# Sums of query and key squares of the first attention from a high and a low part, with later sums and products

## The reference, cut to what matters

```
proj = h @ w_in
qkv = silu(causal_depthwise_conv(proj[..., :3 * A_INNER], conv_w))
q = l2_norm(q) * (A_HEAD_DIM ** -0.5)      # 16 heads of 128 channels
k = l2_norm(k)                             # x * rsqrt(sum(x * x) + eps)
...                                        # beta and decay by token and head
lower = where(tri_strict, einsum(k * beta, k) * decay, 0)     # key-key
qk = einsum(q, k) * decay                                      # query-key
sol = triangular_solve(eye + lower, ...)
```

## Time and profile before

| What | Value |
|---|---|
| Time of the profiled execution | 1381.22 us |
| Its span | 1379.4 us |
| TensorE (PE) busy | 1361.8 us, 99% |
| VectorE (DVE) busy | 973.0 us, 71% |
| ScalarE (ACT) busy | 792.3 us, 57% |
| GpSimd (POOL) busy | 47.2 us, 3% |
| TensorE's share of the chain that ended last | 87% |
| Granted clock of TensorE, mean | 1.00 |
| Bytes moved | 305.80 MB, mean 222 GB/s |

### The profile page before, as it was taken

How to read it: one execution, slowest core, us unless ns; L and a number is a source line. 1 busy time by engine, 2 the same in 40 slices (tenths; PEclk the granted TensorE clock), 3 DMA queues, 4 the chain that set the end, 5 groups by cost and what they waited for, 6 DMA issues and landing times.

```text
span 1379.4 us, 20382 instructions
## 1 busy us (share of the span) xinstructions
PE 1361.8 (99%) x7803; PEld 1158.8 (84%) x7803; DVE 973.0 (71%) x1259; ACT 792.3 (57%) x1021; POOL 47.2 (3%) x93
## 2 busy tenths in 40 slices
PE   6999999999999999999999999999999999999999
PEld 2446999888888888888999988888888888888887
DVE  3568989977787888799765558765666655656552
ACT  2215435465787787745888775467556566466431
POOL 0000022000000000000000000000000000000000
PEclk9999999999999999999999999999999999999999
DMA  9999899856476656474644656645555556555562
GB/s 383 409 417 372 343 379 409 302 188 208 140 264 209 191 182 221 163 237 153 193 149 133 215 175 218 206 163 187 181 183 180 170 171 207 166 175 175 176 191 84
DMA packets 79109, 305.80 MB, mean 222 GB/s; under 512 B 8928, under 2 KB 9328, under 8 KB 74544
## 3 DMA queue, kind: packets, MB, share of 16 engines
q1 hardware_dynamic: 67824, 261.30, 55.1%
q0 software_dynamic: 11200, 43.31, 9.0%
HBM read 294.07 MB, written 12.60 MB: 222 GB/s over the span
## 4 chain that ended last, share of the span: by engine, by line
PE 87%; DMA 6%; DVE 4%; ACT 2%; issue 1%; SPq 0%; POOL 0%; DVEq 0%; ACTq 0%; POOLq 0%
PE acc L713 42%; PE acc L715 21%; DMA raw<-weights 3%; PE acc L738 3%; PE misc L738 3%; PE misc L966 3%; PE acc L657 2%; PE acc L656 2%; PE acc L658 2%; DMA mod_ring<-mod_w 1%; DMA gate_ring<-weights 1%; PE misc L873 1%; DVE w_lo L1604 1%; PE misc L864 1%; DVE gate_ring L1574 1%
## 5 line engine op out<-in xcount | busy, mean ns | idle before, releaser
L713 PE MATMUL acc<-b_op,w_hi 128*128 128x512 f32 x1792 | 635.0, 398 | 0.0
L1604 DVE TENSOR_TENSOR w_lo<-raw,w_hi 128x1024 fp32r<-128x1024 f32 x392 | 470.8, 1221 | 211.6 <-ACT w_hi L1134 206.9
L1134 ACT ACTIVATE w_hi<-raw 128x1024 fp32r<-128x1024 f32 x392 | 404.1, 1053 | 229.7 <-PE acc L715 116.4
L715 PE MATMUL acc<-b_op,w_lo 128*128 128x256 f32 x1792 | 499.6, 279 | 0.0
L713 PEld LDWEIGHTS acc<-b_op,w_hi 128*128 128x128 f32 x1792 | 336.3, 188 | 77.1 <-DVE vo L1648 0.2
L715 PEld LDWEIGHTS acc<-b_op,w_lo 128*128 128x128 f32 x1792 | 337.6, 188 | 0.5
L713 PE MATMUL acc<-a_op,w_hi 128*128 128x512 f32 x760 | 265.0, 395 | 0.3 <-DVEq L1784 0.3
L715 PE MATMUL acc<-a_op,w_lo 128*128 128x256 f32 x760 | 210.8, 277 | 0.0
L713 PEld LDWEIGHTS acc<-a_op,w_hi 128*128 128x128 f32 x760 | 142.5, 188 | 33.8 <-DVEq L1784 0.6
L715 PEld LDWEIGHTS acc<-a_op,w_lo 128*128 128x128 f32 x760 | 142.8, 188 | 0.1
L1574 DVE CUSTOM_DVE_ANT_0 mod_ring<-mod_ring,silu_b,vecs 128x2048 f32<-128x2048 f32 x26 | 61.1, 2350 | 47.6 <-DMA mod_ring<-mod_w 47.4
(11 more groups left out here) (258 smaller groups left out, 1750.1 us busy)
## 6 DMA issues: line engine op xcount, KB each, us to landing
raw<-weights SPq DMA_DIRECT2D x392, 512.0 KB, 4.4
mod_ring<-mod_w SPq DMA_DIRECT2D x26, 1024.0 KB, 13.5
u_ring<-weights SPq DMA_DIRECT2D x32, 512.0 KB, 13.6
gate_ring<-weights POOLq DMA_DIRECT2D x30, 512.0 KB, 8.5
mod_late<-mod_w SPq DMA_DIRECT2D x6, 1024.0 KB, 7.5
xres<-x_t SPq DMA_DIRECT2D x4, 512.0 KB, 15.9
xres<-x_t POOLq DMA_DIRECT2D x4, 512.0 KB, 9.1
sums_b<-sums_d POOLq DMA_DIRECT2D x8, 256.0 KB, 4.6
```

The source lines that it names most:

```text
L713: nc.tensor.matmul(to, w_hi[:, slot, ch], op[:, kt], start=kt == 0, stop=False, skip_group_check=True)
L715: last = nc.tensor.matmul(to[:, 0:T], w_lo[:, slot, ch], op[:, kt, 0:T], start=False, stop=kt == KT - 1, skip_group_check=True)
L1134: nc.scalar.activation(w_hi[:, m.c % HL_SLOTS], raw[:, q.c % RAW_SLOTS], ACT.Copy).then_inc(own.up(s_hi), 1)
L1604: nc.vector.tensor_tensor(w_lo[:, slot], raw[:, q.c % RAW_SLOTS], w_hi[:, slot].bitcast(F32), ALU.subtract).then_inc(own.up(s_lo), 1)
```

## The change

The sums of squares of the queries (c = 0, 2, 4, 6) and of the keys in passes 0 to 2 (c = 1, 3, 5) are made from two fp32r parts. ScalarE copies the squares `t2` to `qk_hi` right behind the Square; VectorE subtracts (heads_low) and writes the rest over `t2` as `t2_lo`; TensorE multiplies both with `ones_r` (sums_of_parts, 4 times hi and lo). The last key sums (c = 7) stay as they were. `ones_r` is made ahead of the passes and no longer ahead of the second attention.

TensorE does the query sums after slab 6 (before: 5) and key_query after slab 3 (2). In passes 0 to 2 it does the key sums after slab 4 (3) and key_key after slab 7 (6); in pass 3 these two stay at 3 and 6. VectorE does the l_t products of passes 0 to 2 in the next pass, behind its first low part; those of pass 3 stay where they were. Its first low part of the second group goes ahead of the product for `q_n`. heads_low stands behind the eviction of the keys' first half (queries), and behind the second low part of the second group (keys).

```diff
+        t2_lo = at("t2_lo", [P, 4 * T], F32R, t2_at)
+        qk_hi = at("qk_hi", [P, 4 * T], F32R, vo_at + 32 * T)
...
-            def split_sums(n):
-
-                pe.wait_ge(s_ones, 1)
-                pe.wait_ge(s_sql, n.v)
+            def sums_of_parts(hi, lo):
+
                 for h in range(BATCH):
                     out, of = misc[:, h * T:(h + 1) * T], slice(h * T, (h + 1) * T)
-                    nc.tensor.matmul(out, ones_r[:], sq_hi[:, of], start=True, stop=False)
-                    last = nc.tensor.matmul(out, ones_r[:], sq_lo[:, of], start=False, stop=True)
+                    nc.tensor.matmul(out, ones_r[:], hi[:, of], start=True, stop=False)
+                    last = nc.tensor.matmul(out, ones_r[:], lo[:, of], start=False, stop=True)
                 last.then_inc(s_nrm, 1)
+
+            def split_sums(n):
+
+                pe.wait_ge(s_sql, n.v)
+                sums_of_parts(sq_hi, sq_lo)
 
             def query_sums(i):
 
                 if i:
                     pe.wait_ge(s_a, i)
-                head_sums(Num(2 * i + 1), t2)
+                else:
+                    pe.wait_ge(s_ones, 1)
+                pe.wait_ge(s_heads_lo, 2 * i + 1)
+                sums_of_parts(qk_hi, t2_lo)
+
+            def key_sums(i):
+
+                if i < 3:
+                    pe.wait_ge(s_heads_lo, 2 * i + 2)
+                    sums_of_parts(qk_hi, t2_lo)
+                else:
+                    head_sums(Num(2 * i + 2), t2)
...
-                fill = {5: lambda: query_sums(i)}
+                fill = {6: lambda: query_sums(i)}
...
-                    fill[2] = lambda: key_query(i - 1)
+                    fill[3] = lambda: key_query(i - 1)
                 joined(g, b_op, fillers=fill)
                 joined(g + 1, b_op, fillers={
-                    3: lambda: head_sums(Num(2 * i + 2), t2), 6: lambda: key_key(i)})
+                    4 if i < 3 else 3: lambda: key_sums(i), 7 if i < 3 else 6: lambda: key_key(i)})
...
                 nc.scalar.activation(t2[:, 0:4 * T], t1[:, 0:4 * T], ACT.Square).then_inc(own.up(s_sq2), 1)
+                if c < 7:
+                    act.wait_ge(*own.last())
+                    nc.scalar.activation(qk_hi[:], t2[:, 0:4 * T], ACT.Copy).then_inc(own.up(s_heads_hi), 1)
...
+            nc.scalar.activation(ones_r[:], ones, ACT.Copy).then_inc(own.up(s_ones), 1)
             for i in range(4):
                 g = G_A + 2 * i
...
-            nc.scalar.activation(ones_r[:], ones, ACT.Copy).then_inc(own.up(s_ones), 1)
             for j in range(4):
...
+            def heads_low(c):
+
+                dve.wait_ge(s_heads_hi, c + 1)
+                nc.vector.tensor_tensor(t2_lo[:], t2[:, 0:4 * T], qk_hi[:].bitcast(F32), ALU.subtract
+                                        ).then_inc(own.up(s_heads_lo), 1)
+
+            def key_products(i):
+
+                dve.wait_ge(s_e, i + 1)
+                for k in range(2):
+                    if i:
+                        dve.wait_ge(s_ld[k], 16 * i)
+                dve.wait_ge(s_kk, i + 1)
+                pair_products(i, l_t, s_l)
...
                 lo_parts(n, 1)
+                if i:
+                    key_products(i - 1)
                 taps(2 * i, t0, t4)
...
                 evicted(2 * i + 1, 0)
+                heads_low(2 * i)
                 lo_parts(n + 4, 2)
                 taps(2 * i + 1, t0, t4, range(0, 2))
                 lo_parts(n + 6, 2)
 
                 n = n + SLABS
                 evicted(2 * i + 1, 1)
+                lo_parts(n, 1)
                 normed_heads(2 * i, q_n)
-                lo_parts(n, 1)
                 if i == 0:
                     sums_in_columns()
                 taps(2 * i + 1, t0, t4, range(2, 4))
                 if i == 3:
                     identity_blocks()
-                lo_parts(n + 1, 4)
+                lo_parts(n + 1, 1)
+                if i < 3:
+                    heads_low(2 * i + 1)
+                lo_parts(n + 2, 3)
                 log_decays(i)
                 normed_heads(2 * i + 1, k_n)
                 evicted(2 * i + 2, 0)
                 lo_parts(n + 5, 2)
-                dve.wait_ge(s_e, i + 1)
-                for k in range(2):
-                    if i:
-                        dve.wait_ge(s_ld[k], 16 * i)
-                dve.wait_ge(s_kk, i + 1)
-                pair_products(i, l_t, s_l)
+                if i == 3:
+                    key_products(i)
                 lo_parts(n + 7, 1)
```

More of the change, by code:

```diff
@@ L243, in program @@
         t1 = at("t1", [P, 4 * T], F32)
+        t2_at = top[0]
         t2 = at("t2", [P, 4 * T], F32)
@@ L440, in program @@
         s_ones = sem("s_ones")
+        s_heads_hi = sem("s_heads_hi")
+        s_heads_lo = sem("s_heads_lo")
         s_sqh = sem("s_sqh")
```

## The result

The changed kernel takes 1385.63 us (median of 20 runs, 1382.66 to 1391.23), the kernel before beside it 1381.23 us (20 runs, 1379.90 to 1383.85). The ratio is 1.0033, interval 1.0026 to 1.0041: slower by 4.4 us. Forecast were 1384.1 and "slower". The profiled execution took 1388.88 us with a span of 1387.1.

A forecast was written before the change was run, and what follows sets the result against it. The prediction took TensorE's stream to bound the kernel: 1381.2 us, less 5.4 for shorter sums, plus 8.3 for waits at the key sums and restarts, gave 1384.1 us, own range 1382.8 to 1385.5 (58%).

The forecast's parts named there:

- The gain: TensorE's sums of squares: 7 of 8 blocks go from 2.07 to 1.30 us, 5.4 us less.
- The loop: Passes 1 to 3, key-query products through VectorE, fetch and ScalarE to key sums: TensorE arrives early and waits.
- The stops: TensorE's waits at the key sums of passes 1, 2 and 3: 2.7, 2.3 and 2.9 us.
- the restart: TensorE resuming after each wait: 0.1 us each, 0.3 us in all.
- Pass 0: Key sums of pass 0, without a key-query block ahead: no wait, 0.4 us to spare.
- The query sums: Low part of the query squares ready at 10.4 us, TensorE there at 10.9: fits by 0.5 us.
- the sum's end: Whole kernel: 1381.2 us less 5.4 for shorter sums plus 8.3 for waits and restarts, 1384.1 us.
- (a): Rival: the fetch lands sooner, ScalarE's waits for it, 3.2 us, can go; 1380.9 us, chance 14%.
- (b): Rival: the loop doesn't bind, only the 5.4 us gain remains; 1375.8 us, chance 13%.
- (c): Rival: TensorE keeps the 0.353 pitch from key sums to key-query and up to 650 us, 2.5 us; 1386.6, chance 15%.
- (d): Rival: the change doesn't do what it says; excluded, as the fp32r form is in the trace.
- Fetch and rule: Slot freed to high part takes 5.75 us; the skill's fit estimates 3.2 for 512 KB, so ScalarE wouldn't wait.

The follow-up runs named there:

- low part first: Changed kernel, key-query still after slab 3, VectorE taking the low part of slab n + 2 ahead of the a_t products in passes 1 to 3: 1377.11 us.
- one stop: Changed kernel with key-query after slab 2 in passes 2 and 3, after slab 3 in pass 1: 1380.39 us.
- key-query at 2: Changed kernel with the key-query block back after slab 2 in passes 1 to 3, all else as changed: 1377.09 us, ratio 0.9961.
- key-query at 2 in the last pass: Changed kernel with key-query after slab 2 in pass 3 only: 1384.66 us, ratio 1.0028.
- the eighth sums: Changed kernel with key-query after slab 2, last key sums also in two parts, after slab 4, key-key after slab 7: 1379.23 us.
- moves alone: Changed kernel with all sums fp32, without copies and subtractions, every sum and product in its new place: 1382.82 us, ratio 1.0011.
- new form alone: Changed kernel's two-part sums with TensorE's blocks and the l_t products in their places of before: 1385.27 us, ratio 1.0029.

## Why the prediction was right

**The gain** was as worked out: blocks of 1.30 us for blocks of 2.07, seven times, 5.4 us, and both kernels without long stops show it as time.

**The loop** was read right, link by link, and it decides. The stops were forecast at 2.7, 2.3 and 2.9 us and are 2.34, 2.28 and 2.70, with 0.1 each for the restart: at the second stop the second product of the sums follows the first (both L886) 520.27 - 519.92 = 0.35 us behind, the next ones 0.23. The 0.4 us too much in pass 1 is the loop itself, 28.48 us where 28.84 was carried over from before. The link that moved is the fetch. From before to after the loops changed by -0.36, -0.01 and -0.22 us, and ScalarE's waits for the fetch by -0.34, -0.02 and -0.23. In the kernel before with key-query at slab 3 that wait grew by 0.72 in pass 1, and the loop by 0.68.

**Pass 0** was to have 0.4 us to spare and has a step of 0.30 us instead of 0.12 (timelines of PE and ACT after; the earlier trace rows is before):

```profile
409.64 0.28 PE L720 MATMUL acc<-b_op,w_lo 128*128 128x256 f32 x1
409.94 0.38 PE L886 MATMUL misc<-qk_hi,ones_r 128*128 128x256 f32 x1
```

```profile
403.00 1.06 ACT L1153 ACTIVATE w_hi<-raw 128x1024 fp32r<-128x1024 f32 x1 [2.13 <-DMA raw<-weights]
```

A miss of 0.6 us on the loop that costs 0.2. It is the fetch again: this high part stands just ahead of the Silu and Square of the keys and now waits 2.13 us for its slab, where before ScalarE waited for no fetch in this pass. The profile of low part first, whose code is the same up to there, has no such wait and no step (0.12 us), that of one stop waits 1.94 us and has none, that of key-query at 2 waits 2.38 us and has 0.53: what goes beyond some 1.95 us becomes the step. So this wait comes and goes with the execution, and the prediction had no term for it. **The query sums** were to fit by 0.5 us: the subtraction ends at 443.75 and they start at 444.33, 0.58 later.

**The step that was mis-sized** is the sum's end, "- 5.4 + 8.3 = 1384.1": it has no term for the clock. 1384.1 - 0.5 (stops) + 2.2 (clock) = 1385.8 against 1385.63. The median lies 0.1 us outside the forecast's own range of 1382.8 to 1385.5, for this reason, and the runs at full clock lie where the forecast is.

**The rivals.** (a), a sooner fetch: refuted, ScalarE still waits 0.92, 0.84 and 0.85 us for it. (The waits are shorter by 0.6 us in sum than in the earlier trace rows, a small part of what (a) claimed, and that is the 0.5 us by which the stops were forecast too long.) (b), the loop doesn't bind: refuted by the stops, and by the kernel before with key-query at 3. (c), the slower pitch: this profile has 1.6 us of it, but after 800 us, where (c) did not put it, and of the seven other kernels with the change's moves or sums only one has it there (below). The table above closes without it. (d) was excluded rightly.

**Fetch and rule.** The sooner fetch that the low part brought gives the price from the other side: where the slot is free in time, ScalarE doesn't wait, and the time falls to 1377.1 us, below rival (a). The Trainium skill (DMA: Bandwidth & Descriptors, section Anatomy of one DMA — SWDGE (gpsimd) path), whose fit gave an estimated 3.2 us for GpSimd's path, would have the slab there in time even in the changed kernel, at an estimated 443.2 us; the trace does not agree: from the low part that frees the slot (438.81 + 1.22) to the high part at 445.43 it is 5.40 us, and ScalarE waits 0.92 of them.

## What to carry to other kernels

When a block on a saturated engine is moved, measure the loop that starts at it: the time from its start through the other engines to the block that waits for their result, against the engine's own work in between. Here 0.6 us to spare became stops of 2.3 to 2.7 us in a place that the moved block doesn't touch, and either one number (key-query a slab sooner) or one reordered low part turned a loss of 4.4 us into a gain of 4. Price a stop of a saturated engine above its length, since the clock may fall behind it: a single one of 2.4 us cost 3.3 here by the medians (11 and 5 runs), with an uncertainty of about 2 us.

## What the hardware showed that was not expected

**The clock can fall when TensorE comes back from a short stop, or in it.** After 440 to 630 us at full clock, a stop of 2.3 to 3 us brought 3.41 us at the half level, in the profiles of the change (from 464.5), of key-query at 2 in the last pass (515.1), of the kernel before with key-query at 3 (461.6) and of the eighth sums (647.6). The fall came between 0.6 us before the engine resumed (461.6 and 462.17) and 1.5 us after (647.6 and 646.12). It doesn't always happen: in the profile of the change the stops of passes 2 and 3, as long as the first, had no fall, and neither had the one-stop kernel's. Runs with a mean clock below 1.000, by the stops of the kernel:

| Longest step at a stop | Stops | Runs below 1.000 |
|---|---|---|
| 0.7 us or less (before, key-query at 2, low part first) | 0 | 0 of 64 |
| 2.1 us (moves alone) | 1 | 0 of 11 |
| 2.5 us (one stop) | 1 | 4 of 11 |
| 3.1 us (the eighth sums) | 1 | 5 of 11 |
| 2.7 us (key-query at 2, last pass) | 2 | 9 of 9 |
| 2.5 us (new form alone) | 3 | 5 of 7 |
| 3.1 us (before, key-query at 3) | 3 | 4 of 5 |
| 2.8 us (the change) | 3 | 14 of 20 |

What decides in a single run is open.

**Two pitches of the same pair.** The stretch of 86.63 us above, from the sums at 815.49 to the L728 at 902.12, takes 85.04 us in the kernel before and as much, to 0.01, in seven of the eight experiments, with the same instructions. The eighth sums have 86.63 again (806.68 to 893.31). Both executions had a fall of the clock before it, but so had two of the others; 1.6 us over some 240 pairs are 0.006 us a pair, the difference between the 0.353 and 0.347 of the earlier trace rows. What sets it was not tried.
